# Token rows by DMA, identity products on TensorE and a fifteenth weight slot in a hybrid decoder step

## What is computed

```python
h = rmsnorm(x, norm_moe)                      # x: 288 tokens after the attention
p_g = softmax(h @ wg + bg); g_sel = argmax(p_g)            # one group of 4
top_p, top_i = top_k(softmax((h @ we + be)[group g_sel]), 2)   # two of its 4 experts
wts = top_p / sum(top_p) * p_g[g_sel]
act = silu(h @ w_gate[e]) * (h @ w_up[e]) * gate[e]        # 16 experts, 2048 -> 512
x = x + act @ w_down[e]                                    # 512 -> 2048
return rmsnorm(x, norm_final)
```

## Time and profile before

| | |
|---|---|
| median of 3 runs | 1483.19 us (1482.83 to 1484.05) |
| the profiled execution | 1484.51 us, its span 1482.8 us |
| PE busy | 1427.7 us (96%) |
| DVE, ACT, POOL busy | 555.9, 190.1, 796.8 us |
| DMA | 377.07 MB, mean 254 GB/s |
| mean granted clock of PE | 0.989 |

### The profile page before, as it was taken

How to read it: one execution, slowest core, us unless ns; L and a number is a source line. 1 busy time by engine, 2 the same in 40 slices (tenths; PEclk the granted TensorE clock), 3 DMA queues, 4 the chain that set the end, 5 groups by cost and what they waited for, 6 DMA issues and landing times.

```text
span 1482.8 us, 25563 instructions
## 1 busy us (share of the span) xinstructions
PE 1427.7 (96%) x9308; PEld 1089.8 (73%) x9308; DVE 555.9 (37%) x1067; ACT 190.1 (13%) x392; POOL 796.8 (54%) x1453
## 2 busy tenths in 40 slices
PE   6999999999999999999999999979999999999997
PEld 6999999998889999998777799963334334344344
DVE  3546578829575342222111342151112122122123
ACT  5100321000000010003222200051000000000003
POOL 3777587979987757763444467512451440522500
PEclk8999999999999999999999999989999999999999
DMA  8344344445654444464788744747999999999993
GB/s 256 124 161 142 107 150 129 155 145 176 208 167 162 142 166 143 146 236 191 299 318 310 248 152 154 293 189 323 421 421 422 422 422 422 422 422 422 422 422 140
DMA packets 106120, 377.07 MB, mean 254 GB/s; under 512 B 12421, under 2 KB 12421, under 8 KB 76290
## 3 DMA queue, kind: packets, MB, share of 16 engines
q1 hardware_dynamic: 103778, 371.68, 65.8%
q10 hardware_dynamic: 2272, 4.42, 0.9%
HBM read 369.30 MB, written 6.77 MB: 254 GB/s over the span
## 4 chain that ended last, share of the span: by engine, by line
PE 83%; DMA 10%; DVE 3%; ACT 2%; issue 1%; SPq 1%; POOL 0%; POOLq 0%; ACTq 0%; DVEq 0%
PE ps L840 40%; PE ps L897 13%; PE ps L1184 11%; DMA tiles<-in_expert_w_up 8%; PE ps L1250 4%; PE ps L1214 3%; PE ps L966 2%; DMA tiles<-in_expert_w_down 2%; PE ps L790 1%; PE ps L1201 1%; PE ps L984 1%; PE ps L974 1%; PE ps L1005 1%; DMA A<-in_norm_final 1%; PE ps L1032 0%
## 5 line engine op out<-in xcount | busy, mean ns | idle before, releaser
L749 POOL COPY A<-A 128x16 f32 x952 | 146.1, 213 | 289.4 <-issue 289.3
L840 PE MATMUL ps<-hT,tiles 128*128 128x144 f32 x1792 | 295.3, 288 | 3.4 <-ACT A L1406 1.5
L840 PE MATMUL ps<-A,tiles 128*128 128x144 f32 x1792 | 262.0, 286 | 0.8 <-DVE A L2003 0.7
L840 PEld LDWEIGHTS ps<-hT,tiles 128*128 128x128 f32 x1792 | 251.6, 191 | 5.0 <-issue 2.6
L840 PEld LDWEIGHTS ps<-A,tiles 128*128 128x128 f32 x1792 | 237.0, 190 | 1.9 <-DVE A L2003 0.9
L702 POOL TENSOR_TENSOR tiles<-tiles 128x512 f32<-128x512 f32 x88 | 117.3, 1333 | 173.4 <-DMA tiles<-in_w_in 70.4
L840 PE MATMUL ps<-tiles 128*128 128x144 f32 x960 | 171.1, 287 | 0.0
L1184 PE MATMUL ps<-tiles,A 128*64 128x512 f32 x512 | 147.0, 601 | 13.2 <-DMA A<-in_expert_w_up 6.4
L840 PEld LDWEIGHTS ps<-tiles 128*128 128x128 f32 x960 | 140.4, 191 | 0.0
L897 PE MATMUL ps<-tiles,mT 128*128 128x256 f32 x512 | 132.9, 382 | 1.0 <-ACT kv_stage L1440 1.0
L1709 DVE COPY pair_sums<-ps 128x144 f32<-128x144 f32 x44 | 13.5, 308 | 300.4 <-PE ps L840 300.4
(11 more groups left out here) (350 smaller groups left out, 1698.6 us busy)
## 6 DMA issues: line engine op xcount, KB each, us to landing
tiles<-in_expert_w_down SPq DMA_DIRECT2D x56, 1024.0 KB, 22.4
tiles<-in_w_in SPq DMA_DIRECT2D x40, 1024.0 KB, 5.1
tiles<-in_expert_w_gate SPq DMA_DIRECT2D x32, 1024.0 KB, 22.1
tiles<-in_expert_w_up SPq DMA_DIRECT2D x32, 1024.0 KB, 22.5
A<-in_expert_w_up SPq DMA_DIRECT2D x24, 1024.0 KB, 25.2
tiles<-in_xa_w_k SPq DMA_DIRECT2D x16, 1024.0 KB, 5.1
tiles<-in_w_out SPq DMA_DIRECT2D x16, 1024.0 KB, 5.1
tiles<-in_xa_w_q SPq DMA_DIRECT2D x16, 1024.0 KB, 5.1
```

The source lines that it names most:

```text
L749: m = nc.gpsimd.tensor_copy(xe[:, :, at + n:at + n + 1], h_moe_or_zero[:, :, bass.ds(token, 1)])
L840: return mm(one(u + mp, x, TH), w[:, kp, mp, :], rhs, start=(first and g == 0 and kp == 0), stop=(g == 3 and kp == 1), skip_group_check=True)
```

## The change

- The tokens are no longer turned. After w_o's end 32 DMAs on the sync queue, between the loads of tiles 9 and 10, copy the rows of `hT` to `h_rows` in the experts' order (`move_rows`). Gate and up weights are read with partition p of group g holding rows 512 g + 4 p to 512 g + 4 p + 3, and row 128 b + p' of `hT` goes to its place there: for each of four quarters `old` and four remainders `new`, 32 partitions. The first 16 DMAs move three of the four groups of blocks, the next 16 the last, each when `h_ready` allows. `rows_moved` counts them. Unused slots copy token 0 in place of a column of zeros.
- 1/rms, which the copies applied, is applied later: PE picks each slot's root with six products of one column (`take_roots`, once before the first branch and once a round), ACT copies them out and scales silu's input by them; for the up branch it is multiplied into the gates on DVE.
- `keep_running`: PE multiplies the identity with weight tiles that are loaded already, six products of 512 columns after the logits and four after the first roots; nobody reads the results.
- `moe_slots` gets a fifteenth buffer, the second half of `mT`. Tiles 0 to 14 of a round go to slots 0 to 14, tiles 15 to 23 to slots 3 to 11; distances are 12 and 24. Tiles 12 and 13 wait for the router's event and the moved rows. `actT` moves to another buffer.
- Of the first job's 64 slots POOL gathers 20 (24 before), ACT 24, DVE 20 (16 before). DVE gathers before it makes counts, gates and jobs; before, it did so after the gates.

```diff
-PE_EVENTS, MOE_SLOTS = 11, 14
+PE_EVENTS, MOE_SLOTS, REUSE = 11, 15, 12
-POOL_SLOTS, ACT_SLOTS = 24, 48
+POOL_SLOTS, ACT_SLOTS = 20, 44
+WARM = 4
...
-            m %= 24
-            return m if m in (12, 13) else m % 12
+            return m % 24 if m % 24 < MOE_SLOTS else m % 24 - REUSE
+
+        def moe_uses(m):
+            return 2 if MOE_SLOTS <= moe_slot(m) + REUSE < 24 else 1
...
-            return 24 if m % 12 < 2 else 12
+
+            return REUSE if m % 24 >= MOE_SLOTS else 24 - REUSE if moe_uses(m) == 2 else 24
...
-        e_gate = a["expert_w_gate"][0].rearrange("e (p g k) f -> e g p k f", k=KT, p=P)
-        e_up = a["expert_w_up"][0].rearrange("e (p g k) f -> e g p k f", k=KT, p=P)
+        e_gate = a["expert_w_gate"][0].rearrange("e (g p k) f -> e g p k f", k=KT, p=P)
+        e_up = a["expert_w_up"][0].rearrange("e (g p k) f -> e g p k f", k=KT, p=P)
...
+                elif m >= 14:
+                    sp.wait_ge(tile_used, TILE["moe"])
                 elif m >= 12:
-                    after_event(sp, EVENT["h_tok_rest"] + 1)
+                    after_event(sp, EVENT["router"])
+                    sp.wait_ge(rows_moved, 16 * 2 * KT * KT)
...
+            def move_rows(first, n):
+
+                sp.wait_ge(h_ready, 4 * HREADY["moe"] + first + n)
+                for old in range(KT):
+                    for new in range(KT):
+                        src = hT[new:P:KT, :, :].rearrange("p (g b) t -> p g b t", b=KT)[:, first:first + n, old, :]
+                        dst = h_rows[P // KT * old:P // KT * (old + 1), :, :].rearrange("p (g b) t -> p g b t", b=KT)[:, first:first + n, new, :]
+                        sp.dma_start(dst, src).then_inc(rows_moved, 16)
+
             branch_tiles(0, 0, range(8))
-            branch_tiles(1, 8, range(MOE_SLOTS - 8))
+            branch_tiles(1, 8, range(2))
+            sp.wait_ge(tile_used, TILE["moe"])
+            move_rows(0, 3)
+            move_rows(3, 1)
+            branch_tiles(1, 8, range(2, MOE_SLOTS - 8))
             sp.wait_ge(jobs_ready, 2)
...
-            pool.wait_ge(tokens_numbered, 2)
-            pool.wait_ge(h_moe_out, 3)
+            pool.wait_ge(rows_moved, 16 * 2 * KT * KT)
             pool.wait_ge(slots_out, 1)
...
+            def keep_running(b, times):
+
+                for n in range(times):
+                    wait_moe_tile(pe, n // KT)
+                    mm(ps[:, b, :], ident[:, :], moe_tile(n // KT)[:, n % KT * TW:(n % KT + 1) * TW], start=True, stop=True)
...
-            for c in range(1, 3):
-                start_unit(pe, UNIT["h_tok"] + c)
-                turn_tokens(c, range(DB)).then_inc(unit_done, 1)
...
-            turn_back_chunk(0, UNIT["h_moe"])
+            keep_running(4 * (UNIT["logits"] % 2), WARM and WARM + 2)
             u = UNIT["places"]
...
+            def take_roots(out):
+
+                for s in range(2):
+                    for c in range(3):
+                        n = own_rows[c]
+                        m = mm(out[:, s:s + 1], pick[0:n, c, C * s:C * s + C], h_rstd[0:n, c:c + 1], start=(c == 0), stop=(c == 2))
+                return m
+
+            pe.wait_ge(tokens_numbered, 1)
+            pe.wait_ge(pick_ready, 1)
+            number_slots(first_slot_sums)
+            take_roots(first_slot_roots).then_inc(unit_done, 1)
...
                 pe.wait_ge(pick_ready, plus(n // 2 + 1, i, 1))
+                take_roots(slot_roots)
                 number_slots(slot_sums)
...
-            turn_back_chunk(1, UNIT["h_moe_rest"])
-            pe.wait_ge(tokens_numbered, 1)
-            pe.wait_ge(pick_ready, 1)
-            number_slots(first_slot_sums)
-            turn_back(2, lambda b: bank(UNIT["places"], 0)[:, b * NB * ST:(b + 1) * NB * ST])
-            read_out(pe, UNIT["h_moe_rest"])
+            keep_running(BRANCH_BANK + 1, WARM)
             read_out(pe, UNIT["places"])
-            pe.wait_ge(h_moe_out, 3)
             pe.wait_ge(xe_ready, 1)
...
-            for c in range(3):
-                tokens_out(c)
-            after_event(act, EVENT["h_moe"])
-            turned_back(0, UNIT["h_moe"])
...
-            def gate_branch(t, s, i):
-
+            def gate_branch(t, s, n, i):
+
+                act.wait_ge(slot_root_out, plus(n, i, 1))
                 after_tile(act, TILE["moe"] + t + 7, i, 24)
-                fn(silu[0:C, :], ps[0:C, 4 + s, :], ACT.Silu).then_inc(silu_ready, 1)
+                fn(silu[0:C, :], ps[0:C, 4 + s, :], ACT.Silu, scale=slot_root[0:C, s:s + 1]).then_inc(silu_ready, 1)
...
             m.then_inc(pick_ready, 1)
+            dve.wait_ge(slots_out, 1)
+            dve.wait_ge(rows_moved, 16 * 2 * KT * KT)
+            for first in range(ACT_SLOTS, C, 16):
+                for n, token in enumerate(tokens_of_slots(mybir.EngineType.DVE, 0, first, min(16, C - first))):
+                    at = first + n
+                    m = v.tensor_copy(xe[:, :, at:at + 1], h_rows[:, :, bass.ds(token, 1)])
+            m.then_inc(xe_third_part, 1)
             after_event(dve, EVENT["counts"])
```

More of the change, by code:

```diff
@@ L75 @@
                ("w_k", 3), ("mix_stat", 1), ("states", 1), ("w_k_last", 1), ("w_out", 8), ("w_q", 8),
-               ("values", 8), ("heads", 2), ("w_o", 8), ("router", 1), ("h_tok", 3), ("h_moe", 1),
-               ("places", 1), ("h_moe_rest", 1), ("final_stat", 1), ("y", 3)):
+               ("values", 8), ("heads", 2), ("w_o", 8), ("router", 1), ("logits", 1),
+               ("places", 1), ("final_stat", 1), ("y", 3)):
     UNIT[_n] = _u
@@ L251, in build @@
         token_no, at = cut(at, 4)
+        actT, at = cut(at, 2, KT, C)
         assert at <= 17088
@@ L447, in build @@
         first_slot_sums = bank(UNIT["places"], 2)[0:1, P:P + 2 * C]
+        first_slot_roots = bank(UNIT["places"], 0)[0:C, 0:2]
+        slot_roots = ps[0:C, 6, T + 4:T + 6]
         def sample_cols(x, lead, per):
@@ L472, in tokens_of_slots @@
             _, tokens = nc.values_load_multi_w_load_instructions(
-                slot_row(p, first, n), engines=[engine], min_val=0, max_val=T,
-                skip_runtime_bounds_check_because="a slot's sum over the tokens holds at most one token's number, 1 to T")
+                slot_row(p, first, n), engines=[engine], min_val=0, max_val=T - 1,
+                skip_runtime_bounds_check_because="a slot's sum over the tokens holds at most one token's number, 0 to T - 1")
             return tokens
@@ L1110, in _ @@
             own_rows = (P, P, NB * ST)
-            def turn_tokens(c, blocks):
-                uc = UNIT["h_tok"] + c
-                for b in blocks:
-                    m = nc.tensor.transpose(bank(uc, b // 4)[0:own_rows[c], b % 4 * P:(b % 4 + 1) * P],
-                                            hT[:, b, c * P:c * P + own_rows[c]], ident[:, :])
-                return m
-            def turn_back(c, out):
-                rows = own_rows[c]
-                pe.wait_ge(h_tok_out, c + 1)
-                for b in range(DB):
-                    m = nc.tensor.transpose(out(b), (h_tok[:, c, :] if c < 2 else h_sam[0:rows, :])[:, b * P:(b + 1) * P],
-                                            ident[0:rows, 0:rows])
-                m.then_inc(unit_done, 1)
-            start_unit(pe, u)
-            for g in range(3):
-                route(g)
-            start_unit(pe, UNIT["h_tok"])
-            turn_tokens(0, range(12))
-            route(3).then_inc(unit_done, 1)
-            turn_tokens(0, range(12, 16)).then_inc(unit_done, 1)
+            start_unit(pe, u)
+            for g in range(4):
+                m = route(g)
+            m.then_inc(unit_done, 1)
+            def keep_running(b, times):
+                for n in range(times):
+                    wait_moe_tile(pe, n // KT)
+                    mm(ps[:, b, :], ident[:, :], moe_tile(n // KT)[:, n % KT * TW:(n % KT + 1) * TW], start=True, stop=True)
+            u = UNIT["logits"]
+            start_unit(pe, u)
             pe.wait_ge(logits_in, 1)
@@ L1545, in slots_numbered, with roots_out @@
                 copy(slot_row(p, 0, 2 * C), sums).then_inc(slots_out, 1)
-            act.wait_ge(token_rstd_ready, 1)
-            for c in range(3):
-                tokens_out(c)
-            after_event(act, EVENT["h_moe"])
-            turned_back(0, UNIT["h_moe"])
+            def roots_out(roots):
+                copy(slot_root[0:C, :], roots).then_inc(slot_root_out, 1)
             act.wait_ge(gate_in, 2)
@@ L2064, in _ @@
             v.tensor_copy(rstd[:, 0, :], bank(u, 0)[:, 0:T]).then_inc(logits_in, 1)
+            dve.wait_ge(logits_in, 1)
+            dve.wait_ge(stat_out, 1)
+            dve.sem_inc(half_free[u % 2], 2)
+            u = UNIT["logits"]
             dve.wait_ge(token_root, 1)
@@ L2116, in _ @@
             then(tt(G(11), G(11), G(14), ALU.add))
+            then(tt(G(11), G(11), h_rstd[:, 0:3].unsqueeze(2).broadcast_to([P, 3, 4]), ALU.mult))
             for c in range(3):
```

83 lines of the change are left out of this document (29 added, 54 removed).

## The result

The kernel was to become 9.0 us faster, and became 21.2 us slower.

A forecast was written before the change was run, and what follows sets the result against it. The prediction took the DMA stream of experts' weight tiles, started by PE's first branch, as the bound; 5.7 + 1.7 + 1.6 = 9.0 us off 1484.5 gave 1475.5, as a median 1474.2, range 1471 to 1480.5.

The forecast's parts named there:

- Start of the branch: PE's first expert branch, at 999.24 before: to start at 993.5, 5.7 us earlier, with tokens no longer turned.
- PE's own line: PE ahead of the first branch: numbering until 987.3, root products 1.3, four identity products, ready at 993.8.
- I take 0.5: Sync queue's issue of the 32 row DMAs: 0.5 us each, last issued at 984.2, rows there at 986.8, cost 0.
- rival 1: Rows land last at 0.65 us an issue or slower moving: branch at 996.9, time 1477.6 to 1479.3; chance 0.17.
- The moving itself: DMA engines moving 2.36 MB of rows within SBUF: 9 us, between 5.6 and 12, shorter than the issuing.
- rival 2: Rows gate everything: at 1.01 us an issue, branch at 1008.0, 7.2 us slower, 1490.4; chance 0.08.
- The clock: First branch's first group on PE: identity products keep the clock up, worth 1.7 us, between 0 and 1.7.
- The fifteenth slot: Experts' weight stream: one tile of 2.49 us fewer to load, less 0.9 of idle DMA, net 1.6 us.
- The stream's other condition: Sync queue's wait for DVE's job list: 999.7 plus about 0.5 for register loads, need 1000.4; cost 0, bound 1.
- Root products in the rounds: Twelve records a round on PE: 1.3 us, 10.4 over eight rounds, paid by spare time; cost 0.
- tiles left to load x 2.49: Experts' stretch: time is stream start plus tiles left at 2.49 us each plus tail, 421 GB/s to the end.
- The gathers change hands: First 64 slots' gathers split POOL 20, ACT 24, DVE 20; DVE's 20 take 5.1 us, reaching PE at 993.1.

The follow-up runs named there:

- e4: The changed kernel with twelve more small memsets on POOL and ACT's roots copy ahead of its gathers: 1480.63 us, kernel before 1483.87, ratio 0.9979.
- e10: e7 with four and two identity products in place of six and four: 1476.45 us, kernel before 1483.73, ratio 0.9950.
- e3: The changed kernel with ACT's copy of the roots and its signal ahead of ACT's 56 gathers: 1499.78 us, ratio to the kernel before 1.0108.
- e7: e4 with half of the 32 row transfers issued by POOL: 1477.38 us, kernel before 1483.16, ratio 0.9955.
- e1: The changed kernel with twelve more small memsets on POOL after its first gathers: 1485.24 us, kernel before 1483.87, ratio 1.001.
- e6: e4 with no identity products: 1480.00 us, kernel before 1483.16, ratio 0.9972.
- the fastest version: e10, timed twice: 1476.45 us, kernel before 1483.73; again as e12, 1476.19 us, kernel before 1484.42.
- e9: e7 with no identity products: 1480.27 us, kernel before 1483.73, ratio 0.9971.
- e11: e10 with 14 weight slots in place of 15, on one chip with e12: 1478.34 us, kernel before 1484.42, ratio 0.9962.
- e12: e10 unchanged, timed again on one chip with e11: 1476.19 us, kernel before 1484.42, ratio 0.9950.
- e5: e4 with 14 weight slots in place of 15: 1481.44 us, kernel before 1483.16, ratio 0.9983.
- e8: The kernel before with 56 more small memsets on POOL after its first gathers: 1483.26 us, kernel before 1483.16, ratio 0.9999.
- e2: The kernel before with 112 more small memsets on POOL after its first gathers: 1505.10 us, kernel before 1483.87, ratio 1.0150.

## Why the prediction was wrong, step by step

**Start of the branch: predicted 5.7 us earlier; after, 2.6 later by distance; with the roots first and the fetches gone (e4) 3.1 earlier; with rows from two queues and fewer identity products (e10) 4.9.** The places and the slot numbers came as said (980.2 and 985.0, 14.5 and 19.3 us after the first row transfer; predicted 13.8 and 19.0). Three steps failed behind them. (1) "PE's own line" and the gathers were taken for all that the branch waits for. A third condition stands in the code, PE's and DVE's wait for the bank with the roots, and its signal was behind 56 gathers on ACT. I had asked who waits for ACT's new wait, but for the silu alone, and priced it at nothing. It cost 5.0 us (e3). (2) "I take 0.5" for an issue. It was 0.65 from one to the next (21.79 / 32 is 0.68; 0.64 in the later part), the price that rival 1 named; rows landed at 988.7, 23.0 us after the first issue in place of 18.1, and the gathers began 5 us after the slot numbers. With half the issues on another queue (e7, e10) they begin as soon as the numbers and the registers are there. But that alone did not move the branch (e7: 28.1 us after the first row transfer). (3) "PE's own line" was 25.1 us in the forecast and too short: the identity products behind the roots, taken at 5.2 us, ran 6.66 us in e4, at half clock for the most part, and ended 27.0 us after the first row transfer in e4 and 28.1 in e7. With two products fewer in each group (e10) the branch came 2.4 us earlier.

**The moving itself** was taken at 9 us (5.6 to 12). Three stretches in which one queue's row transfers are all that the engines carry: 970 to 974 and 974 to 980 in the changed kernel, 974 to 977 in e4:

```profile
970.00:974.00 4.00, 3.11 (x30) 2.09 (x24) 0.96 (x5) 2.23 (x6) 0.00 (x0) 0.99 0.52 166
974.00:980.00 6.00, 6.00 (x11) 2.49 (x10) 4.54 (x31) 1.30 (x3) 0.00 (x0) 0.72 0.96 147
```

```profile
974.00:977.00 3.00, 3.00 (x8) 1.33 (x8) 2.40 (x17) 1.54 (x2) 0.00 (x0) 1.00 0.60 183
```

The same pieces of 1152 bytes don't have one price. A share of 0.96 at 147 GB/s is 153 GB/s for full engines, against 421 for tiles, and 2.36 MB would be 15.4 us by that, over my upper end; 0.60 at 183 is 305 GB/s and 7.7 us. With two queues at work it is 216 GB/s at a share of 1.05 (e10, 970 to 974), 11.5 us. So 9 us is neither borne out nor refuted, and what makes the pieces twice as dear in one stretch as in another is not shown. Behind issues of 21 us it stayed hidden, as forecast. The Trainium skill (SBUF — State Buffer, Door 1: The DMA port swizzle) would give a transfer whose partitions reach 8 of the 16 ports half of the rate, 210 GB/s as an estimate from 421; here the destination is 32 neighbouring partitions, the source 32 that are four apart. The stretch with two queues is close to that, the others don't decide it. The Trainium skill's other rule (DMA: Bandwidth & Descriptors, Rules for kernel authors: under 64 KB mostly overhead) is not borne out in the form of rival 2: transfers of 108 and 36 KB cost the queue 0.6 us alike, not 1.01.

**The clock: 1.7 us.** In the changed kernel the clock was down in the first group in spite of the products, which end at 992.3; PE then stood for 6.5 us. But how long PE stood is not what decides: in e1, the same program for PE, it stood for 4.3 us and its first pairs ran at full clock,

```profile
998.63 0.64 PE L1199 MATMUL ps<-tiles,A 128*64 128x512 f32 x1 [4.30 <-ACTq L1585]
```

and in e10 it stood for 1.6 us and they ran at half (1.08). In e4, where PE hardly stands, the first pairs are at 0.61; but there the products can be left out with no loss that can be measured (e6), since the list decides. In the fastest version, where PE decides, leaving them out costs 3.8 us by the medians (e9 against e10), over my upper end of 1.7. In the two profiles 1.9 of 3.1 us lie behind the first products: I had left out the places, which run at the low clock without them. (The numbering, 1.52 us, runs at half clock in both.)

**The fifteenth slot: 1.6 us**, measured 2.2 (e11, e12), 0.6 to 1.5 (e4, e5), and 0.5 to 2.5 by the length of the stream in the profiles. Right within what can be told.

**The stream's other condition: cost 0, bound 1.** "About 0.5 (an estimate)" for the sync queue's register loads was the wrong term: they are 3.78 us, in three kernels alike. (In the kernel before, the same five loads run from 1002.29, 0.03 us after the list, to 1005.5, when PE's tiles were not yet used.) POOL's 16 registers in one load were a poor row for it; the queue loads the number of rounds and the experts one by one. So even in the kernel before the list was not 5.7 us ahead of need (1008.03) but 2.0: 1002.26 + 3.78 = 1006.04. Once the branch moves by more than that, the list is the bound, and it cost e4 2.9 us: by PE's need the stream would start 6.9 us after the branch, at 1000.6, and it starts at 1003.48. In the changed kernel, where ACT's signal holds both, the list (1002.87 + 3.78 = 1006.65) is not the last; PE's half clock is.

**Root products in the rounds: 1.3 us, covered.** A round's twelve take 1.07 us. At PE's own pace a round became 0.9 us longer (56.6 in place of 55.7), and one that is held by loads is as long as before where there are no fetches (59.66 in e1 too). Right.

```profile
1088.56 1.07 PE L1177 MATMUL ps<-mT,A 128*64 128x1 f32 x12
```

**The term that failed most: "tiles left to load x 2.49", at 421 GB/s to the end, with nothing charged for the instructions themselves.** "The gathers change hands" had its cost in DVE's and ACT's time and none in what POOL gives up. Taking nine instructions out ahead of a loop was priced at nothing, as all removals were; it brought five fetches into each round, a tile then took 62.95 / 24 = 2.62 us in place of 2.49, and it cost 19.6 us. What hint there was stands in the profile of before: its q14 line with 22 fetches, none of them from 1060 to 1440, says that POOL's loop was kept, and a stretch with the engines at 1.01 has no room for one engine's extra work. None of the rivals had it; rival 2 had the sign and the wrong cause.

**Sum.** 5.7 + 1.7 + 1.6 = 9.0 was forecast. e4, the change with ACT's order and the fetches mended, has 3.2. Its stream starts 5.4 us later than forecast: 2.6 of a branch that starts late, held by late rows and, to within 0.5 us, by the identity products, and 2.9 of the list and its loads. The fastest version has 7.3 to 8.2. So the chain at the seam was right in its places and slot numbers, and wrong in one wait that it left out (ACT's signal, 5.0 us in the kernel as it was) and in three prices: an issue, 0.5 for 0.65; the queue's register loads, 0.5 for 3.78; the identity products at the low clock.

## What to carry to other kernels

In a stretch where all DMA engines are full, look at the instruction queues of the profile: a few fetches a round weigh on one engine alone, and the slowest engine sets when every tile lands. Adding or removing instructions of an engine ahead of its loop can make the loop be fetched anew in every round; count fetches per round before and after, and pad if they appear. For each signal that the path's end waits for, read what stands ahead of it in its engine's program, however small the instruction that gives it. And a queue that reads a list into registers before it issues has a price of its own, which shows in no busy time.

## What the runs showed of the hardware

**A loop of POOL is kept or fetched anew by where it lies.** The loop has 277 instructions in all kernels here. Where it starts in the kernel before is 0 below; it starts at +4 in e1 (twelve memsets and a wait on top of the change), +21 in e7, +57 in e8, -9 in the changed kernel and +113 in e2. From 1060 to 1440 there are 0 to 2 fetches at 0, +4, +21 and +57, and 32 and 29 at -9 and +113, five a round, of 8 KB each. Nine instructions lie between the nearest two of either kind. With instructions of 64 bytes, as the Trainium skill says (Trainium Architecture — The Big Picture, The software stack), 8 KB are 128 instructions, and +113 is 15 short of 128. Then all six starts fit one rule, no fetches while the loop touches three blocks of 128 and all refetched when it touches four, provided that a block begins in the nine instructions up to the start of the kernel before's loop. Where blocks begin is not shown; that place is fitted, and the rule is a reading of six points. Nor does it say why there are five fetches for four blocks. The Trainium skill (Runtime: NRT & Kernel Launch, Instruction fetch mechanics) gives an engine's memory 512 instructions in two pages of 256, and warns of branches that leave it for the stall of the engine. Here the engine hardly stalls (0.19 us a round) and the pieces are half as large; the loss is on the DMA side.

**What a fetch costs.** A round was 3.3 us longer with five fetches. 41 KB more for one engine are 1.6 us at 26.3 GB/s, so a fetch costs its engine about 0.66 us, twice its bytes. Why twice, stays open. That all fall on one engine is read from the end of the stream (18 GB/s at a share of 0.05), in two kernels.

**Transfers within SBUF**, from 32 partitions four apart to 32 neighbouring ones: 0.59 to 0.61 us of the sync queue's time each and 0.65 from one to the next, for 108 KB and for 36 KB alike, against 0.33 to 0.35 for a tile of 1 MB; POOL issued 16 in 9.12 us, 0.57 each. From one queue they ran at 147 GB/s at a share of 0.96 and at 183 at 0.60; with two, at 216 at a share of 1.05 (e10, 970 to 974).

**Register loads of the sync queue**, the number of rounds and the experts, took 3.78 us from the list's last value to the first tile's issue, the first of them 0.49.
